# Second layer norm by token tile, weight and bias applied behind the transposition, root of the mean square passed on to tables, epilogues and value rows

## The reference, cut to what matters

```
x = layer_norm(ALPHA * x + nsa_mixer(x), ln_g[1], ln_b[1])     # second layer norm
h = x * rsqrt(mean(x * x) + 1e-6) * ln1                        # root-mean-square norm
dq, dk, dv, sq, sk, sv = split(h @ w_in)                       # 6 x 1024 columns
q1, q2, k1, k2 = partial_rotary(dq), ..., partial_rotary(dk)   # q * cos + turned(q) * sin
...
x = x + mixed @ w_out                                          # needs x itself again
```

## Time and profile before

| what | value |
|---|---|
| median of 3 runs | 2146.78 us (2145.99 to 2147.34) |
| the profiled execution, its own time | 2147.38 us |
| its span in the profile | 2145.6 us |
| PE busy | 2063.8 us, 96% of the span |
| DVE busy | 1285.7 us, 60% |
| ACT busy | 969.4 us, 45% |
| POOL busy | 66.6 us, 3% |
| mean granted clock of PE | 0.987 |
| HBM | 167 GB/s over the span |

### The profile page before, as it was taken

The page is one execution under the profiler, slowest core; times in us unless marked ns, Lnnn a source line. Parts: engine busy times, 40 slices in busy tenths (PEclk is TensorE's granted clock), DMA queues, the critical chain, the costliest instruction groups (busy, mean ns, idle before and its releaser), DMA issues.

```text
span 2145.6 us, 32731 instructions
## 1 busy us (share of the span) xinstructions
PE 2063.8 (96%) x12774; PEld 1807.3 (84%) x12774; DVE 1285.7 (60%) x1746; ACT 969.4 (45%) x1397; POOL 66.6 (3%) x78
## 2 busy tenths in 40 slices
PE   8999999999999999888999999899999999999997
PEld 7898798988888898768889887788888888888886
DVE  6798765466565666566555655566555555655654
ACT  5554444344444444334345545544434434434443
POOL 2000021000000000000000000100000000000000
PEclk9999999999999999998999999999999999999999
DMA  8334576645454545553545544455566566556552
GB/s 270 99 109 169 170 216 206 171 132 170 135 166 137 166 138 162 199 171 109 166 125 161 158 119 156 166 181 183 198 194 187 192 192 189 183 200 192 187 196 89
DMA packets 199537, 359.86 MB, mean 168 GB/s; under 512 B 21488, under 2 KB 30000, under 8 KB 198768
## 3 DMA queue, kind: packets, MB, share of 16 engines
q1 hardware_dynamic: 197616, 352.01, 52.7%
q0 software_dynamic: 1600, 5.96, 0.9%
q10 hardware_dynamic: 192, 0.05, 0.0%
HBM read 355.88 MB, written 2.10 MB: 167 GB/s over the span
## 4 chain that ended last, share of the span: by engine, by line
PE 53%; issue 38%; DVE 6%; ACT 2%; POOL 0%; DMA 0%; ACTq 0%; DVEq 0%; POOLq 0%
PE acc L484 23%; PE acc L488 19%; PE acc L566 1%; DVE w_low L1645 1%; ACT w_high L1068 1%; PE banks L812 1%; PE banks L898 1%; PE banks L841 1%; PE banks L767 1%; PE banks L629 1%; PE banks L827 0%; PE banks L917 0%; PE banks L550 0%; PE banks L901 0%; PE banks L836 0%
## 5 line engine op out<-in xcount | busy, mean ns | idle before, releaser
L1645 DVE TENSOR_TENSOR w_low<-raw,w_high 128x1024 fp32r<-128x1024 f32 x648 | 792.6, 1229 | 677.3 <-ACT w_high L1068 675.7
L1068 ACT ACTIVATE w_high<-raw 128x1024 fp32r<-128x1024 f32 x648 | 683.2, 1059 | 775.5 <-PE acc L484 341.9
L488 PE MATMUL acc<-x_high_low,w_high 128*128 128x256 f32 x2432 | 359.4, 287 | 2.0 <-issue 2.0
L484 PE MATMUL acc<-w_high,x_high_low 128*128 128x512 f32 x1152 | 323.9, 394 | 3.9 <-ACT transposed_tmp L1453 3.9
L488 PEld LDWEIGHTS acc<-x_high_low,w_high 128*128 128x128 f32 x2432 | 321.2, 194 | 4.2 <-issue 3.0
L484 PEld LDWEIGHTS acc<-w_high,x_high_low 128*128 128x128 f32 x1152 | 211.6, 188 | 47.2 <-issue 3.7
L488 PE MATMUL acc<-x_high_low,w_low 128*128 128x256 f32 x1216 | 196.7, 284 | 0.0
L484 PE MATMUL acc<-w_high,h_high 128*128 128x512 f32 x560 | 175.7, 395 | 6.3 <-DVE w_low L1645 3.7
L484 PE MATMUL acc<-w_low,x_high_low 128*128 128x512 f32 x576 | 178.3, 391 | 0.0
L484 PE MATMUL acc<-w_low,h_high 128*128 128x512 f32 x560 | 173.8, 392 | 0.0
L484 PE MATMUL acc<-w_high,h_low 128*128 128x512 f32 x560 | 173.6, 391 | 0.0
(11 more groups left out here) (358 smaller groups left out, 2157.7 us busy)
## 6 DMA issues: line engine op xcount, KB each, us to landing
raw<-in_b_w_in SPq DMA_DIRECT2D x128, 512.0 KB, 3.7
raw<-in_w_mlp_in SPq DMA_DIRECT2D x128, 512.0 KB, 3.7
raw<-in_w_mlp_out SPq DMA_DIRECT2D x128, 512.0 KB, 3.6
raw<-in_w_in SPq DMA_DIRECT2D x96, 512.0 KB, 4.1
raw<-in_kv_w SPq DMA_DIRECT2D x48, 512.0 KB, 4.3
raw<-in_a_w_in SPq DMA_DIRECT2D x32, 512.0 KB, 4.9
raw<-in_b_w_out SPq DMA_DIRECT2D x32, 512.0 KB, 4.2
raw<-in_w_out SPq DMA_DIRECT2D x32, 512.0 KB, 3.6
```

Of the source, the lines that this page charges most:

```text
L484: ins_ = nc.tensor.matmul(PAIRS[pair][:, t, :], xa[:, kt + j, t * P:(t + 1) * P], wa[:, k, j, :], start=first and n == 0, stop=last and n ...
L488: ins_ = nc.tensor.matmul(ACC[pair][:, m // 2, (m % 2) * TOK:(m % 2 + 1) * TOK], wa[:, k, j, m * P:(m + 1) * P], xa[:, kt + j, :], start=f ...
L1068: nc.scalar.activation(WH[:, s % SPLIT, :, :], RAW[:, s, :, :], ACT.Copy).then_inc(hi_ready, SLOTS + 1 if first_one else 1)
L1645: V.tensor_tensor(WL[:, k, :, :], RAW[:, p % SLOTS, :, :], WH[:, k, :, :].bitcast(F32), ALU.subtract).then_inc(lo_ready, SLOTS + 1 if isin ...
```

## The change

- The last unit of U_BOUT is done as U_AOUT is: 4 ticks as before, the last 4 by token tile, and `layer_norm` on DVE is the code of the first layer norm, now called twice. `whiten` and `turned` go.
- Weight and bias behind the transposition are ln_g[1]·ln1 and ln_b[1]·ln1, in row 1 of the parameter columns. Two small DMAs, one transposition of 32 columns (in the first attention group's lead-in) and two small DVE products prepare them early.
- `natural` on DVE writes weight and bias into x in rows, one piece of 128x512 (a product and a sum) after each of 8 splits of units U_QKV and U_QKV+1; `row_square` on ACT squares each piece one split later.
- `root`, POOL, `root_diagonals` (DVE), `root_columns` (PE: ones times the diagonal), `rotary_tables` (DVE: cos and sin times the root) come in ticks 3 to 5 of U_QKV+1. `rotary(0)` on DVE moves from tick 1 to tick 5 of that unit; `rotate(0)` on PE stays at tick 1.
- Kinds 2 and 5 are multiplied by the root in `half_copy`; kinds 3 and 4 are now both halves on DVE, with the root's columns. The lambda steps move into unit U_QKV+2.

```diff
+NATURAL = [0, 1, 2, 3, 4, None, None, None, 5, 6, 7] + [None] * 5
+SQUARED = [None, 0, 1, 2, 3, None, None, None, 4, 5, 6, 7] + [None] * 4
@@ PE
+        pe.wait_ge(ln_cols_in, 32)
+        nc.tensor.transpose(BK[2][:, P:P + 32], PR[0:32, 1, :], ID[0:32, 0:32])
...
-        for u in range(4):
+        for u in range(3):
             gemm(U_BOUT + u, G_BOUT + u, "rows", HH, HL,
-        transposes(TR_H, HN, lambda i: pe.wait_ge(rows_ready, 5 + i // 2))
+        pe.wait_ge(acc_free, G_BOUT + 2)
+        for s in range(SPLIT):
+            tick((U_BOUT + 3) * SLOTS + s, s, "rows", (G_BOUT + 3) % 2, 2 * s, s == 0, False, HH, HL)
+        tiles_apart(U_BOUT + 3, (G_BOUT + 3) % 2, 2 * SPLIT, False, HH, HL)
+        for b in range(4):
+            tile_turn(TR_H, 0, b, 8)
+        for b in range(2):
+            tile_turn(TR_H, 1, b, 8)
+        def root_columns():
+            pe.wait_ge(root_diag, 1)
+            for t_ in range(NT):
+                ins_ = nc.tensor.matmul(BK[3][:, t_ * P:(t_ + 1) * P], const("ones"), RD[:, t_, :], start=True, stop=True)
+            ins_.then_inc(root_cols, 1)
...
+                if n == 0 and s in (1, 3):
+                    tile_turn(TR_H, 1, 2 + s // 2, 8)
                 if s == 1 and kind in (1, 2):
                     rotate(2 * j + kind - 1)
+                if n == 1 and s == 5:
+                    root_columns()
@@ ACT
-        for c in range(4):
-            act.wait_ge(x_rows, c + 1)
-            squares(c)
-        turned(TR_H, gain=32)
+        for m in range(8):
+            tile_turned(TR_H, m, 1, 0, 16)
+            if m in (3, 5, 6):
+                high(0)
+        def row_square(i):
+            t, c = divmod(i, 4)
+            act.wait_ge(x_rows, i + 1)
+            if i:
+                act.wait_ge(row_squares, i)
+            nc.scalar.activation(SQR[:, :], X[:, t, c * COLS:(c + 1) * COLS], ACT.Square, accum_out=CS[:, t, c:c + 1]).then_inc(row_squares, 1)
...
+                if n < 2 and SQUARED[8 * n + s] is not None:
+                    row_square(SQUARED[8 * n + s])
@@ DVE
-        for c in range(4):
+        for c in range(3):
             low(0, SLOTS)
             residual(SLOTS * (U_BOUT + c + 1), (G_BOUT + c) % 2, c, ALPHA)
             chunk_stats(c, G_BOUT + c)
-        v.wait_ge(gain_in, 96)
-        whiten(3)
+        low(0, SLOTS - LEAD)
+        layer_norm(1, G_BOUT + 3, U_QKV, TR_H)
+        def natural(i):
+            t, c = divmod(i, 4)
+            ...
+            if c == 0:
+                v.wait_ge(tr_full, TR_H + 4 + 4 * t)
+            steps.link(V.tensor_tensor(xr, xr, GB2[:, 0, cols], ALU.mult))
+            V.tensor_tensor(xr, xr, GB2[:, 1, cols], ALU.add).then_inc(x_rows, 1)
+        def rotary_tables():
+            v.wait_ge(root_cols, 1)
+            steps.link(V.tensor_copy(RR[:, :], BK[3][:, 0:TOK]))
+            for name in ("cos", "sin"):
+                steps.inc(V.tensor_tensor(const(name), const(name), RR[:, :], ALU.mult))
+            steps.wait()
...
+                ins_ = V.scalar_tensor_tensor(dst, ACC[(G_QKV + n) % 2][:, b, :].rearrange("p (m t) -> p m t", m=2),
+                                              HD ** -0.5 if kind == 3 else 1.0, RR[:, :].unsqueeze(1).to_broadcast([P, 2, TOK]),
+                                              ALU.mult, ALU.mult)
...
+                if n < 2 and NATURAL[8 * n + s] is not None:
+                    natural(NATURAL[8 * n + s])
+                if n == 1:
+                    if s == 3:
+                        root()
+                    if s == 4:
+                        root_diagonals()
+                    if s == 5:
+                        rotary_tables()
+                        rotary(0)
+                if n == 2 and s == 0:
+                    lambda_sums()
+                if n == 2 and s == 4:
+                    lambdas()
@@ POOL
+        for i, name in enumerate(("ln_g", "ln_b")):
+            pool.dma_start(PR[16 * i:16 * i + 16, 1, :], tiles(ins[name][1])).then_inc(ln_cols_in, 16)
...
-        rsqrt(3)
-        rsqrt(4)
+        rsqrt(3, 0, 1)
+        rsqrt(4, 1, 2)
+        rsqrt(5)
```

More of the change, by code:

```diff
@@ L1355, in _, with tile_turned @@
         unit()
-        def tile_turned(first, m, gain, bias):
+        def tile_turned(first, m, row, gain, bias):
             t, b = TURN_ORDER[m]
@@ L1565, in beside @@
                     second_stage("sb", j - 1, 8 * kind + s)
-            unit(first=(lambda n=n: qkv_epilogue(n - 1)) if n else None, extras=beside)
+            unit(first=(lambda n=n: qkv_epilogue(n - 1)) if n else None, extras=beside, ticks=SLOTS if n else SLOTS - 3)
         for n in range(12):
@@ L2145, in _ @@
         v.wait_ge(gate_full, 2)
+        for i in range(2):
+            ins_ = V.tensor_tensor(PT[:, 1, 16 * i:16 * i + 16], BK[2][:, P + 16 * i:P + 16 * i + 16], PT[:, 0, 32:48], ALU.mult)
+            if i:
+                ins_.then_inc(ln_cols, 1)
+            else:
+                steps.inc(ins_)
         steps.link(V.tensor_scalar(GATE[:, :, :].rearrange("p t n -> p (t n)"), BK[2][:, 0:NT * GATES], 1.0, 0.25, ALU.add, ALU.mult))
@@ L2498, in _ @@
         v.wait_ge(gain_in, 112)
-        root_mean_squares(5, 12, None)
+        v.wait_ge(row_squares, 16)
+        steps.link(V.tensor_reduce(MS[:, NT:2 * NT], CS[:, :, :], AX_X, ALU.add))
+        V.tensor_scalar(MS[:, 0:NT], MS[:, NT:2 * NT], 1.0 / DM, NORM_EPS, ALU.mult, ALU.add).then_inc(ms_rows, 1)
+        v.wait_ge(rstd_rows, 6)
+        for c in range(4):
+            cols = slice(c * COLS, (c + 1) * COLS)
+            for t in range(NT):
+                V.scalar_tensor_tensor(X[:, t, cols], X[:, t, cols], RSTD[:, t:t + 1], GF[:, cols],
+                                       ALU.mult, ALU.mult).then_inc(out_ready, 1)
     @block.gpsimd
```

188 lines of the change are left out of this document (88 added, 100 removed).

## The result

| | before | changed |
|---|---|---|
| median, us | 2146.74 (2145.99 to 2147.34, 4 runs) | 2129.52 (2128.55 to 2131.79, 4 runs) |
| profiled execution, us | 2147.38 | 2129.16 |
| its span, us | 2145.6 | 2127.4 |
| its mean granted clock | 0.987 | 0.993 |

The ratio is 0.9923, 95% interval 0.991 to 0.9935: faster by 17.2 us. The forecast was 2132.2 us, 2.7 us too slow, inside the range.

A forecast was written before the change was run, and what follows sets the result against it. It took PE, busy 96% of the time, as the bound, with a longest single wait of 18.9 us. Terms -15.10 + 0.4 + 0 + 0 + 0.1 = -14.6 us gave a median of 2132.2 us, range 2129.0 to 2137.0.

The forecast's parts named there:

- The transition, -15.10 us: U_BOUT's last product to U_QKV's fifth tick: 36.41 us becomes 21.31, as at the first layer norm.
- Natural pieces at nothing: Weight and bias pieces on DVE beside U_QKV and U_QKV+1 ticks: 2.7 us of PE's 2.88, so no cost.
- Root's matmuls +0.4: Two float32 matmuls on PE behind tick 5 of U_QKV+1: 0.4 us, bounds 0.2 and 0.9.
- Kinds 3 and 4 on DVE: Four units with two DVE passes each instead of one: 0 us, bounds -0.3 and +1.5.
- small products: Combined weights: PE's transposition of 32 columns costs 0.1 us, bounds 0 and 0.3; small products lie units ahead of use.
- lambda: The lambda steps, 5 small operations, are off the path.
- The clock at 0 with bounds of 3.5: Granted clock at the transition and in later attention drops: bounds -3.5 and +3.5 us.
- rival 2: Clock stays up through the transition or a later drop falls away: 1.8 to 3.5 us more gain; 10 in 100.
- The root was not late: Rival: DVE's copy, tables and rotation end after PE's tick 7, or loaded ticks lag: 1 to 5 us back; 15 in 100.
- The gain was whole: Rival: the transition shortens less, second tile's pieces come late: half the gain, 2140 us; 4 in 100.
- rival 4: Rows, squares and splits run in series in loaded ticks, pieces 4.4 us apart: slower, 2148.4 us; 2 in 100.

The follow-up runs named there:

- run 9: run 3's kernel with sixteen waits for counts long reached, adding eight instructions on TensorE ahead of the MLP's loop; 2148.58 us, ratio 1.0008.
- run 2: The changed kernel with U_BOUT's last unit in four ordinary ticks for both tiles, not tile by tile; 2136.43 us, ratio 0.996.
- run 3: The kernel before, with only the by-tile order added; weight, bias and root stay ahead of the transposition; 2156.75 us, ratio 1.0048.
- Run 6: The changed kernel with the two weight and bias passes on each natural piece cut to one column; 2130.93 us, ratio 0.9929.
- run 4: The changed kernel with all eight natural pieces together behind the first split of U_QKV, not one after each split; 2140.38 us, ratio 0.9976.
- run 5: The changed kernel with the two weight and bias passes on each natural piece done twice; 2140.52 us, ratio 0.9972.
- run 7: The changed kernel with the root's matmuls, tables and first rotation one tick later; 2137.1 us, ratio 0.9954.
- run 10: The changed kernel with TensorE's MLP loop written out three times; 2129.34 us, ratio 0.9921.
- run 11: The changed kernel with the first piece of tile 1 handed over in halves in both norms and TensorE's MLP loop written out; 2126.32 us, ratio 0.9906.

## Why the prediction was right, and where its size was off

**The transition, -15.10 us: right.** 953.52 (953.12 + 0.40) to the fifth tick at 974.55 is 21.03 us for 21.31 forecast, so -15.38. The copy of the first norm's stretch holds, as function and order were the same; its idle times, 2.08 and 2.38, answer to 2.02 and 1.97 of the earlier trace rows. The second is 0.4 longer only because the eight transpositions ahead of it end earlier (1.08 us for 1.49, at a higher clock): from their start to the first tick it is 3.46 us in both. The excess over four ticks and two groups is 1.50 us for 1.84.

**What the transition's gain is made of**, by the runs: order by tile with weight, bias and root still ahead of the transposition +1.8 us (run 9 against the before beside it), these moved behind it but PE's last ticks not by tile -9.8 (run 2 likewise), both -17.2. Moving them carries it, and only behind that do PE's last ticks by tile pay, 6.7 us. The prediction took the two as one and did not say so. No run moves the root alone or weight and bias alone. Run 3's DVE rows give an estimate: per tile some 4.0 us (5.9 less 1.92) for weight and bias and 2.7 for squares' sum, root and normed_rows, so both are needed for the gain.

**Natural pieces at nothing: right, by a margin.** 2.7 us a loaded tick was forecast and 2.46 came, since the three passes follow each other closer (0.72, 0.61 and 1.14 us from start to start) than the rows' own lengths and a wait say. Run 6 shows the zero, runs 4 and 5 what it costs when the cover is gone.

**Root's matmuls +0.4: right.** 1005.12 to 1005.48 is 0.36 us. From them to the end of the rotation DVE took 5.97 us (forecast 5.93), PE had 6.20 (6.16), and the margin is 0.23 us (0.2). Run 7 shows that it is a real margin.

**Kinds 3 and 4 on DVE, small products, lambda: no trace of them above 0.5 us.** Beside its slow stretches the low parts of the weights drift by 0.2 us over the attention. Its wait for probs_first grew from 0.7 to 1.4 us in all.

**The clock at 0 with bounds of 3.5: mis-sized.** Two of the attention's three slow stretches, the one at 0.66 of the earlier trace rows and its neighbour at 1075, are absent in three profiles of the changed kernel of three: -2.0 us. This is the case of rival 2, which the prediction gave 10 in 100 and which names 2128.7 to 2130.4; the five executions of the fourteen at 0.990 or 0.991 may have such a stretch again. A further 2.4 us is ahead of the transition, and as far as the profiles tell that is luck: 1.4 of it in the first 93 us, 0.5 in the ticks behind the first norm (0.93 in place of 0.86 of the clock from 240 to 265), 0.5 in the blocks up to 750. TensorE's code is the same there in runs 5, 7 and 10, whose profiles are 1.6 to 2.1 us later than the changed kernel's at 281 us, near before's 1.9. Against it stands a term that no row of before could show, the return of the MLP's loop, +0.9 us. Together, in the profiled pair: -14.9 - 2.0 - 2.4 + 0.2 + 0.9 = -18.2, all of it, where the prediction has -14.6. So the transition and what stands beside it were forecast to 0.3 us, and the surplus is clock and chance, in part cancelled by the loop.

The Trainium skill (TensorE: Matmul & The Clock Gate, "What's actually happening") ties the higher level to activity, and the prediction doubted that two gaps of 2 us would leave the clock up. The trace lies between: it fell, to 0.75 from 957.35 to 964.17.

**The rivals.** The root was not late. The gain was whole. The series of rows, squares and splits (rival 4) did not come: the pieces stand 2.46 us apart and not 4.4.

## What to carry to other kernels

A norm's weight, bias and root need not stand ahead of the transposition and the product that follow: apply weight and bias where they are per-partition columns, and pass the root on to where the product is read. The engine that would wait then loses only the pieces' own latency. Price a moved stretch by a stretch of the same trace that already runs the new order, and then look for where its cover ends (here 0.42 us a tick and 0.23 us at the rotation), since a wait of TensorE cost 1.3 to 1.7 times its length on the spot, the clock included (9.2 for 7.05, 10.0 for 5.8 and 4.4 for 2.54 us in runs 4, 5 and 7). Count no more of the clock than the profile's own place shows: stretches that come and go elsewhere made up to 4 us between two profiles. Before a slower variant is put down to its idea, look for idle "issue" time at a loop's start far from the edit: here two such gaps made a neutral edit look 10 us slower.

## What the runs showed of the hardware

**The return of a long loop.** The trace has the branch at the MLP loop's end on TensorE's sequencer (instruction: shortest, median and longest ns, starts), of the changed kernel; the shortest is the last, which falls through:

```profile
L1077 PEldq COMPARE_BRANCH  x3: 83/3644/4816, 1756.4 to 2110.5; - x3
```

In all twelve profiles that have this branch (runs 10 and 11 don't) the two returns took 3.6 to 4.8 us. It shows little: in the changed kernel TensorE works on for 4.1 us behind the branch's start, and over the profiles it is idle for 0 to 1.0 us a return, but for run 3. The attention's loop, with 1,372 records of TensorE between two branches where the MLP's has 1,873, returns in a quarter of a microsecond:

```profile
L877 PEldq COMPARE_BRANCH  x3: 76/212/244, 547.6 to 770.5; - x3
```

The trace also shows code being fetched. A DMA queue of the kind "instruction" (q8) moves packets of 16 KB. In the attention's loop, from 548 to 771, the changed kernel has no packet of it; in one pass of the MLP's loop, from 1756.44 to 1933.93, it has nine, two of them within 7 us of the branch:

```profile
q8 instruction: 9, 0.15, 0.3%
```

Over the whole run these packets are 95 in the changed kernel and 91 with that loop written out (run 10), where none falls between 1757 and 1765. So the return of the longer loop has its code brought again, and that of the shorter one does not.

Run 3 stopped four instructions behind the loop's start, with nothing left in the queue to hide it, for 5.0 and 3.8 us; eight instructions' shift removed both (run 9). In the first of these gaps, between 1778.9 and 1782.9, there is one more such packet:

```profile
q8 instruction: 1, 0.02, 1.5%
```

That a packet's worth of code ended there and TensorE stood until the next had come is the reading that this row and run 9 bear out; where the packets' bounds lie in the program was not looked up. The Trainium skill (Runtime: NRT & Kernel Launch, "Instruction fetch mechanics") says that a taken branch to a page not at hand forces a fetch "before execution can continue", which agrees, and that the crossing of a boundary is mostly hidden, which holds in a line (run 10) and did not hold right behind a return (run 3).

**A short wait and the clock.** One wait of 2.54 us with full work on both sides was followed by a granted clock of 0.73 from 1016 to 1020, in a stretch that has 1.00 without it; wait and clock together cost 4.4 us (run 7). The low clock of some later stretches, with TensorE all but busy, can't be put to such a wait: from 1055 to 1100 it is 0.92 in before and in runs 3 and 9, 0.96 in runs 2, 4 and 7, and 1.00 in the others. What decides it is open.
